# A transformer step's MoE combine: who normalizes the first two tiles, and two rows from TensorE to VectorE

## The chip, the core and the metric

The kernel runs on one core of a Trainium2 chip. A core has five engines that work beside each other: TensorE (PE, matmuls), VectorE (DVE), ScalarE (ACT), GpSimd (POOL) and SyncE (SP, which here issues DMAs). Each runs its own list of instructions in order and waits for the others on semaphores. The metric is the device time of one execution in microseconds (us), as a median of several runs.

## What is computed

The reference is one step of a two-layer backbone on 384 tokens of 1024 numbers: 128 context tokens and 256 latent ones. Each layer has a mixer and a mixture of experts. What the change touches is the end of the second:

```python
xp = _layernorm(ALPHA * xp + mp[5] * _moe(_modulate(xp, mp[3], mp[4]), *mw), ln2_g[l], ln2_b[l])
xs = _layernorm(ALPHA * xs + ms[5] * _moe(_modulate(xs, ms[3], ms[4]), *mw), ln2_g[l], ln2_b[l])

def _layernorm(x, g, b):
    mu = xf.mean(-1, keepdims=True)
    var = jnp.square(xf - mu).mean(-1, keepdims=True)
    y = (xf - mu) * lax.rsqrt(var + LN_EPS) * g + b
...
```

`_moe` sends each token to 8 of 64 experts; its result for a token is the sum of 8 expert rows, each times a weight, and a shared expert's row. In layer 0 what comes next is the mixer of layer 1, which needs the normalized x and its modulated form h, both from the same mean and variance with different scales and shifts. In the last layer the normalized x is the output.

## The kernel before

The tokens are three tiles of 128 (tile 0 is the context). The kernel is written as a sequence of stages; inside a stage each engine has a program written out by hand, and at a stage's end all engines meet. `stage_moe` joins four such programs per engine: routing, experts, overflow and, last, the combine (`combine_programs`, from L3272), once for each layer.

The combine works in this order.

- SP loads the expert rows of each tile back from DRAM (`y_rows`) in six parts, two a tile (L3331). In layer 0 it then loads the first chunks of the next stage's weights, as their places come free (`ahead`). In the last layer it stores the three finished tiles (L3336).
- TensorE sums rows in PSUM banks: first what was placed on chip (L3352), then for each tile some of its 8 rows, each as a product with a diagonal matrix of the weights (L3359), and at the end the part that VectorE summed, as a product with the identity (L3364). Which rows are whose is in the tables `DVE_ROWS` and `PE_ROWS` (L3262). Before, VectorE has 6, 4 and 3 rows of tiles 0, 1 and 2, and TensorE 2, 4 and 5. In layer 0 TensorE then turns tile 0 and tile 1 (`pe_turn_tile`, L1963), runs the first product of the next stage for tile 0 (L509), turns tile 2, and runs tile 1's product.
- VectorE adds its rows into `cat`, each step waiting for the one before (`add_rows`, L3407). `residual(t)` multiplies the sum in PSUM with the gate, in two halves (L3419), and adds it to ALPHA * x (L3422, or L3425 for tile 2). For tiles 0 and 1 this step also gives the sum for the mean (L3428). `centred(t)` is (x + minus mean) * scale over 128x1024 (L3436), and `scaled(t)` is that times rstd plus the shift (L3447), with the result h in `hP`, or in the last layer in x. L3440 makes the variance from the squares, L3449 the small term for the normalized x.
- ScalarE writes the diagonals (L3383) and sums the squares of tiles 0 and 1 (L3388). In layer 0 it copies each turned tile (L1970) and then normalizes x in place (Identity with scale and bias, L3396).
- GpSimd only computes rstd, a power of minus one half on 128x1 (`pool_rstd`, L1941).

Semaphores on the way: `s_mu` mean ready, `s_sq` squares ready, `s_v` variance, `s_p` rstd, `s_h` output of a tile ready (TensorE's turn and SP's store wait for it), `s_sum` and `s_took` for the PSUM banks.

Of the kernel before, what the change touches and what calls it, by code (L numbers as in the profile page):

```python
# [283 lines left out]
def sems(nc, ctx, names):  # L284
    found = [ctx.enter_context(nc.semaphore(n)) for n in names.split()]
    ctx.used += found
    return found
# [2973 lines left out]

DVE_ROWS = ((0, 1, 4, 5, 6, 7), (0, 1, 4, 5), (0, 1, 4))  # L3262
PE_ROWS = tuple(tuple(j for j in range(TOPK) if j not in DVE_ROWS[t]) for t in range(TILES))
# [8 lines left out]
def combine_programs(k, layer, ctx, s_over, s_fold, n_fold, tables, ends, ahead=None):  # L3272
# [34 lines left out]
    def in_place(eng, t, j):  # L3307
# [6 lines left out]
        nc, ctx, "cb_row_added cb_steps cb_var cb_rstd cb_shift cb_h cb_turned outputs_stored")  # L3314
    s_mu, s_sq = sems(nc, ctx, "cb_mean cb_squares")
    squares = k.s[:, 1440:1440 + D]
# [24 lines left out]
    def on_gpsimd(pool):  # L3341
        nc.gpsimd.drain()
        for t in range(TILES):
            pool_rstd(k, M, pool, t, s_v, s_p)

    def on_tensor(pe):
# [33 lines left out]
    def on_scalar(act):  # L3380
        for t in range(TILES):
            for i, j in enumerate(PE_ROWS[t]):
                m = nc.scalar.mul(diag[:, rows_before(PE_ROWS, t) + i, :], k.ident, k.w8[:, t, j:j + 1])  # L3383
            m.then_inc(s_dg, 1)

        def squares_of(t):
            act.wait_ge(s_mu, t + 1)
            nc.scalar.activation(squares, k.x[:, t, :], ACT.Square, bias=M.mv[:, t, 0:1], accum_out=M.mv[:, t, 1:2]).then_inc(s_sq, 1)  # L3388

        squares_of(0)  # L3390
        squares_of(1)
        for t in range(0 if last else TILES):
            x = k.x[:, t, :]
            copy_turned(k, act, t, turn_banks[t], s_tr).then_inc(s_hT, 1)
            act.wait_ge(s_nb, t + 1)
            nc.scalar.activation(x, x, ACT.Identity, bias=M.nb[:, t:t + 1], scale=M.mv[:, t, 1:2])  # L3396

    def on_vector(dve):
        st = Steps(dve, s_d)
        st.mark(nc.vector.memset(M.half, -0.5))  # L3400

        def add_rows(t):
            for i, j in enumerate(DVE_ROWS[t]):
                n = rows_before(DVE_ROWS, t) + i
# [26 lines left out]

        def centred(t):
            G = tables.scale[min(t, 1)]
            if t < SUMMED_BY_ACT:
                dve.wait_ge(s_mu, t + 1)
            st.mark(nc.vector.scalar_tensor_tensor(k.cat[:, t, :], k.x[:, t, :], M.mv[:, t, 0:1], G,  # L3436
                                                   ALU.add if t < SUMMED_BY_ACT else ALU.subtract, ALU.mult))
            if t < SUMMED_BY_ACT:
                dve.wait_ge(s_sq, t + 1)
                nc.vector.tensor_scalar(M.mv[:, t, 1:2], M.mv[:, t, 1:2], 1.0 / D, LN_EPS, ALU.mult, ALU.add).then_inc(s_v, 1)  # L3440

        def scaled(t):
            rstd = M.mv[:, t, 1:2]
            B, out = tables.shift[min(t, 1)], k.x[:, t, :] if last else k.hP[:, t, :]
            st.wait()
            dve.wait_ge(s_p, t + 1)
            nc.vector.scalar_tensor_tensor(out, k.cat[:, t, :], rstd, B, ALU.mult, ALU.add).then_inc(s_h, 1)  # L3447
            if not last:
                nc.vector.tensor_scalar(M.nb[:, t:t + 1], M.mv[:, t, 0:1], rstd, 1.0 if t < SUMMED_BY_ACT else -1.0,  # L3449
                                        ALU.mult, ALU.mult).then_inc(s_nb, 1)  # L3450

        add_rows(0)
        add_rows(1)
        residual(0)
        centred(0)
        residual(1)
        scaled(0)
        centred(1)
        add_rows(2)
        scaled(1)  # L3460
        residual(2)
        centred(2)
        scaled(2)

# [153 lines left out]
```

## Time and profile before

| what | us |
|---|---|
| median of 3 runs (lowest, highest) | 1723.14 (1720.74, 1725.92) |
| the profiled execution | 1723.91 |
| its span, first to last instruction | 1722.0 |
| busy in it: PE, PE weight loads | 1564.6, 739.4 |
| busy in it: DVE, ACT, POOL | 588.9, 368.5, 239.0 |
| combine of layer 0: VectorE's first row, TensorE's first product of the next stage | 883.01, 919.69 |
| combine of the last layer: VectorE's first row, its last step's start | 1677.16, 1717.40 |

The rest of this text reads the trace of the profiled execution. A row of the timeline is: start, duration, engine, line of the kernel, operation, output and inputs by name, their shape, and in brackets for how long the engine had been idle before it and what it waited for. PE's granted clock was 0.961 of full speed over the span.

### The profile page before, as it was taken

The numbers are of one execution on the slowest core, as the hardware profiler recorded it, in microseconds if no ns is written. First come the engines' busy times: TensorE is split into PE (matmuls) and PEld (weight loads), VectorE is DVE, ScalarE is ACT, GpSimd is POOL, SyncE is SP. The second block draws the span as 40 slices with busy tenths as digits, with TensorE's granted clock in tenths as the row PEclk, the third lists the DMA queues.
The fourth block names the chain that finished last, engine by engine and source line by source line (L and its number), as shares of the span: only waits on it lengthen the run. The fifth ranks groups of instructions, "written<-read, shape, count | busy, mean of one in ns | idle before, by whom it ended". The sixth has DMA issues, their size and how long they took to land. (4 is left out here: it accounts for less than half of the span.)

```text
span 1722.0 us, 19372 instructions
## 1 busy us (share of the span) xinstructions
PE 1564.6 (91%) x6918; PEld 739.4 (43%) x6918; DVE 588.9 (34%) x1432; ACT 368.5 (21%) x798; POOL 239.0 (14%) x223
## 2 busy tenths in 40 slices
PE   4999889996898999999999889998698999899987
PEld 1666644542343344344334744533243444344423
DVE  2333685532223111111146675632123111111117
ACT  2224621211111111121224272111011111111121
POOL 0010121111111123111100000111111122211100
PEclk8999999998899999999999999999899999999999
DMA  9990388699999999999983106699999999999974
GB/s 384 374 359 12 137 342 355 244 420 422 399 401 419 400 380 411 396 406 419 380 360 128 62 21 273 270 372 420 412 386 411 389 391 386 406 411 401 400 316 187
DMA packets 110819, 579.55 MB, mean 337 GB/s; under 512 B 22042, under 2 KB 24730, under 8 KB 52480
## 3 DMA queue, kind: packets, MB, share of 16 engines
q1 hardware_dynamic: 87584, 526.61, 75.5%
q0 software_dynamic: 22560, 50.00, 7.6%
q10 hardware_dynamic: 576, 1.66, 0.3%
q8 instruction: 57, 0.93, 0.2%
q14 instruction: 42, 0.34, 0.1%
HBM read 563.77 MB, written 45.30 MB: 354 GB/s over the span
## 5 line engine op out<-in xcount | busy, mean ns | idle before, releaser
L3093 DVE TENSOR_TENSOR scratch<-scratch,bank 128x256 f32<-128x256 f32 x84 | 51.5, 614 | 590.0 <-ACT scratch L3046 561.4
L2952 PE MATMUL bank<-weights,scratch 128*64 128x512 f32 x384 | 185.7, 632 | 52.3 <-DMA scratch<-in_moe_w_up 41.9
L2952 PE MATMUL bank<-scratch 128*64 128x512 f32 x352 | 174.1, 644 | 23.1 <-DMA weights<-in_moe_w_up 14.0
L2953 PE MATMUL bank<-weights,scratch 128*64 128x512 f32 x384 | 190.4, 641 | 0.0
L2953 PE MATMUL bank<-scratch 128*64 128x512 f32 x384 | 185.3, 636 | 0.0
L3046 ACT ACTIVATE scratch<-bank 128x256 f32<-128x256 f32 x84 | 32.2, 383 | 571.5 <-PE bank L2953 355.6
L2952 PEld LDWEIGHTS bank<-weights,scratch 128*64 128x64 f32 x384 | 52.9, 145 | 163.9 <-issue 161.7
L2657 POOL DMA_INDIRECT y_rows<-hP,y_idx x39 | 41.5, 1064 | 448.2 <-ACT hP L3054 330.0
L2952 PEld LDWEIGHTS bank<-scratch 128*64 128x64 f32 x352 | 48.8, 146 | 124.6 <-issue 122.8
L2642 POOL DMA_INDIRECT hP<-h_rows,tok_idx x78 | 81.3, 1043 | 132.8 <-PE bank L2603 66.3
L2959 PE MATMUL bank<-weights,scratch 128*128 128x512 f32 x224 | 98.4, 592 | 0.0
L2959 PE MATMUL bank<-scratch 128*128 128x512 f32 x224 | 98.4, 592 | 0.0
L2990 PE MATMUL bank<-weights,scratch 128*64 128x512 f32 x192 | 87.5, 598 | 2.0 <-ACT scratch L3050 2.0
L2991 PE MATMUL bank<-weights,scratch 128*64 128x512 f32 x192 | 87.5, 599 | 0.0
L2991 PE MATMUL bank<-scratch 128*64 128x512 f32 x192 | 87.5, 599 | 0.0
L2019 PE MATMUL bank<-scratch,cat 128*128 128x512 f32 x192 | 83.7, 594 | 4.1 <-ACT cat L1681 3.4
L2657 POOL DMA_INDIRECT y_rows<-z,y_idx x37 | 39.0, 1055 | 345.2 <-ACT z L3054 269.2
L2990 PE MATMUL bank<-scratch 128*64 128x512 f32 x176 | 80.2, 598 | 3.1 <-ACT scratch L3050 3.1
L2603 PE MATMUL bank<-const,hP 128*128 128x128 f32 x624 | 81.1, 273 | 0.5 <-DMA hP<-h_rows,tok_idx 0.5
L2603 PEld LDWEIGHTS bank<-const,hP 128*128 128x128 f32 x624 | 70.4, 141 | 3.8 <-DMA hP<-h_rows,tok_idx 2.2
L3098 DVE COPY hP<-bank 128x512 f32<-128x512 f32 x40 | 27.7, 692 | 121.7 <-PE bank L2991 121.7
L2959 PEld LDWEIGHTS bank<-scratch 128*128 128x128 f32 x224 | 42.6, 190 | 53.5 <-issue 53.5
(411 smaller groups left out, 2444.5 us busy)
## 6 DMA issues: line engine op xcount, KB each, us to landing
weights<-in_moe_w_gate SPq DMA_DIRECT2D x62, 1024.0 KB, 12.6
weights<-in_moe_w_up SPq DMA_DIRECT2D x62, 1024.0 KB, 20.0
weights<-in_moe_w_down SPq DMA_DIRECT2D x62, 1024.0 KB, 20.6
scratch<-in_moe_w_gate SPq DMA_DIRECT2D x60, 1024.0 KB, 11.9
scratch<-in_moe_w_up SPq DMA_DIRECT2D x60, 1024.0 KB, 20.2
scratch<-in_moe_w_down SPq DMA_DIRECT2D x60, 1024.0 KB, 20.9
weights<-in_w_mod SPq DMA_DIRECT2D x6, 2048.0 KB, 11.3
wmod_more<-in_w_mod SPq DMA_DIRECT2D x6, 2048.0 KB, 8.6
```

Of the source, the lines that this page charges most:

```text
L2019: m = nc.tensor.matmul(k.ps[2 * t + c][:], cat[:, kk, t * P:(t + 1) * P], w_half[c][kk // (KT // 2)][:, kk % (KT // 2), :], start=(kk == 0 ...
L2603: m = k.nc.tensor.transpose(k.ps[kk // 4][:, (kk % 4) * P:(kk % 4 + 1) * P], B.xg[:, b, kk * P:(kk + 1) * P], k.ident)
L2642: return k.nc.gpsimd.indirect_dma_start(out=out, out_offset=None, in_=table, in_offset=bass.IndirectOffsetOnAxis(ap=idx, axis=0), bounds_c ...
L2657: return k.nc.gpsimd.indirect_dma_start(out=table, out_offset=bass.IndirectOffsetOnAxis(ap=idx, axis=0), in_=in_, in_offset=None, bounds_c ...
L2952: nc.tensor.matmul(out[0:HALF, :], x[:, 0:HALF], w0[:, kk], start=(kk == 0), stop=(kk == KT - 1))
L2953: m = nc.tensor.matmul(out[HALF:P, :], x[:, HALF:P], w1[:, kk], start=(kk == 0), stop=(kk == KT - 1))
L2959: m = nc.tensor.matmul(out[:], x, w[:, kk], start=(kk == 0), stop=(kk == KT - 1))
L2990: nc.tensor.matmul(k.ps[5 + c][0:HALF, :], h[:, 0:HALF], w0[:, j, cols], start=(j == 0), stop=(j == 1))
L2991: m = nc.tensor.matmul(k.ps[5 + c][HALF:P, :], h[:, HALF:P], w1[:, j, cols], start=(j == 0), stop=(j == 1))
L3046: nc.scalar.activation(B.ex[b % 2], k.ps[2 + b % 2][:, 0:FD], ACT.Silu).then_inc(s_e, 1)
L3093: nc.vector.tensor_tensor(B.h[b % 2].rearrange("p (j q) -> p q j", j=2), B.ex[b % 2].rearrange("p (q j) -> p q j", j=2), k.ps[2 + b % 2][: ...
L3098: nc.vector.tensor_copy(y_out(b, slice(512, 1024)), k.ps[6][:]).then_inc(s_yv, 1)
```

## The change

For tiles 0 and 1, the two wide VectorE steps `centred` and `scaled` are gone. Instead ScalarE computes the small term (`nb`, minus mean times rstd), waits for it, and normalizes x in place, in both layers; GpSimd multiplies that by the scale and then adds the shift, each over 128x1024, with a semaphore between (`s_xn`, `s_xs`). Tile 2 stays as it was (`normed_last`). VectorE takes one row more of tile 1 and one more of tile 2 (6, 5, 4), TensorE one less of each (2, 3, 4), and VectorE's order is another: the rows of tile 2 come in two pairs around the variance of tile 0, ahead of `residual(1)`. ScalarE's copies of turned tiles come after both normalizations.

```diff
-DVE_ROWS = ((0, 1, 4, 5, 6, 7), (0, 1, 4, 5), (0, 1, 4))
+DVE_ROWS = ((0, 1, 4, 5, 6, 7), (0, 1, 4, 5, 6), (0, 1, 4, 5))
...
         for t in range(TILES):
             pool_rstd(k, M, pool, t, s_v, s_p)
+            if t < SUMMED_BY_ACT:
+                pool.wait_ge(s_xn, t + 1)
+                nc.gpsimd.tensor_tensor(k.cat[:, t, :], k.x[:, t, :], tables.scale[min(t, 1)], ALU.mult).then_inc(s_xs, 1)
+                pool.wait_ge(s_xs, t + 1)
+                nc.gpsimd.tensor_tensor(k.x[:, t, :] if last else k.hP[:, t, :], k.cat[:, t, :], tables.shift[min(t, 1)], ALU.add).then_inc(s_h, 1)
...
-        squares_of(0)
-        squares_of(1)
+        for t in range(SUMMED_BY_ACT):
+            x, rstd = k.x[:, t, :], M.mv[:, t, 1:2]
+            squares_of(t)
+            act.wait_ge(s_p, t + 1)
+            nc.scalar.mul(M.nb[:, t:t + 1], M.mv[:, t, 0:1], rstd).then_inc(s_nb, 1)
+            act.wait_ge(s_nb, t + 1)
+            nc.scalar.activation(x, x, ACT.Identity, bias=M.nb[:, t:t + 1], scale=rstd).then_inc(s_xn, 1)
         for t in range(0 if last else TILES):
+            copy_turned(k, act, t, turn_banks[t], s_tr).then_inc(s_hT, 1)
+        if not last:
+            t = TILES - 1
             x = k.x[:, t, :]
-            copy_turned(k, act, t, turn_banks[t], s_tr).then_inc(s_hT, 1)
...
         add_rows(0)
         add_rows(1)
         residual(0)
-        centred(0)
+        add_rows(2, 0, 2)
+        variance(0)
+        add_rows(2, 2)
         residual(1)
-        scaled(0)
-        centred(1)
-        add_rows(2)
-        scaled(1)
+        variance(1)
         residual(2)
-        centred(2)
-        scaled(2)
+        normed_last()
```

VectorE in the last layer's combine, before, from the mean of tile 0 (L3428) to the rows of tile 2 (L3407):

```order
L3428 TENSOR_SCALAR z<-z 128x1
L3436 SCALAR_TENSOR_TENSOR cat<-x_tok,z,scratch 128x1024
L3440 TENSOR_SCALAR z<-z 128x1
L3419 TENSOR_TENSOR cat<-bank,z 128x512
L3422 SCALAR_TENSOR_TENSOR x_tok,z<-x_tok,cat 128x512
L3419 TENSOR_TENSOR cat<-bank,z 128x512
L3422 SCALAR_TENSOR_TENSOR x_tok,z<-x_tok,cat 128x512
L3428 TENSOR_SCALAR z<-z 128x1
L3447 SCALAR_TENSOR_TENSOR x_tok<-cat,z,scratch 128x1024
L3436 SCALAR_TENSOR_TENSOR cat<-x_tok,z,scratch 128x1024
L3440 TENSOR_SCALAR z<-z 128x1
L3407 SCALAR_TENSOR_TENSOR cat<-scratch,cat 128x1024 x3
```

So each tile's centring and scaling stood on VectorE between the residual steps, and tile 2's rows came after the residual step of tile 1.

The same place in the changed kernel; its L3440 is the mean, L3446 the variance, L3419 a row, L3431 and L3434 the two halves of a residual step:

```order
L3440 TENSOR_SCALAR z<-z 128x1
L3419 SCALAR_TENSOR_TENSOR cat<-scratch,cat 128x1024 x2
L3446 TENSOR_SCALAR z<-z 128x1
L3419 SCALAR_TENSOR_TENSOR cat<-scratch,cat 128x1024 x2
L3431 TENSOR_TENSOR cat<-bank,z 128x512
L3434 SCALAR_TENSOR_TENSOR x_tok,z<-x_tok,cat 128x512
L3431 TENSOR_TENSOR cat<-bank,z 128x512
L3434 SCALAR_TENSOR_TENSOR x_tok,z<-x_tok,cat 128x512
L3440 TENSOR_SCALAR z<-z 128x1
L3446 TENSOR_SCALAR z<-z 128x1
```

Three wide steps (two L3436, one L3447) are gone from between the residual steps, and tile 2's rows, now four, stand ahead of the residual step of tile 1 where three stood behind it.

GpSimd in layer 0's combine, before: the three powers follow each other.

```order
L2657 DMA y_rows<-hP,scratch 3072x1024
L3197 UNCONDITIONAL_BRANCH
L1941 TENSOR_TENSOR z<-z 128x1 x3
L274 UNCONDITIONAL_BRANCH
L562 UNCONDITIONAL_BRANCH
L566 MEMSET z 128x64
L274 UNCONDITIONAL_BRANCH
```

GpSimd had nothing else in this stretch.

And in the changed kernel; L3347 is the product with the scale, L3349 the sum with the shift:

```order
L2657 DMA y_rows<-hP,scratch 3072x1024
L3197 UNCONDITIONAL_BRANCH
L1941 TENSOR_TENSOR z<-z 128x1
L3347 TENSOR_TENSOR cat<-x_tok,z 128x1024
L3349 TENSOR_TENSOR hP<-cat,z 128x1024
L1941 TENSOR_TENSOR z<-z 128x1
L3347 TENSOR_TENSOR cat<-x_tok,scratch 128x1024
L3349 TENSOR_TENSOR hP<-cat,scratch 128x1024
L1941 TENSOR_TENSOR z<-z 128x1
L274 UNCONDITIONAL_BRANCH
```

Two wide steps stand between the powers of tiles 0 and 1, and two between those of tiles 1 and 2.

## Rows read from the trace of the kernel before

**Rows 1.** The page's head: span and number of instructions.
```profile
span 1722.0 us, 19372 instructions
```

**Rows 2.** Groups by line and shape, VectorE's rows: count, busy us, mean ns, idle us.
```profile
L3407 DVE SCALAR_TENSOR_TENSOR cat<-scratch,cat 128x1024 f32<-128x1024 f32 x14 | 18.0, 1283 | 1.3
```

**Rows 3.** Timeline of the last layer's combine, VectorE and GpSimd's powers: start, duration.
```profile
1677.16 2.68 DVE L3407 SCALAR_TENSOR_TENSOR cat<-weights,scratch,cat 128x1024 f32<-128x1024 f32 x2
...
1685.51 5.45 DVE L3407 SCALAR_TENSOR_TENSOR cat<-weights,scratch,cat 128x1024 f32<-128x1024 f32 x4
1691.67 0.69 DVE L3419 TENSOR_TENSOR cat<-bank,z 128x512 f32<-128x512 f32 x1 [0.72 <-PE bank L3364]
...
1696.36 0.56 POOL L1941 TENSOR_TENSOR z<-z 128x1 f32<-128x1 f32 x1 [41.48 <-DVE z L3440]
...
1705.66 4.06 DVE L3407 SCALAR_TENSOR_TENSOR cat<-scratch,cat 128x1024 f32<-128x1024 f32 x3
1705.83 1.52 POOL L1941 TENSOR_TENSOR z<-z 128x1 f32<-128x1 f32 x1 [8.91 <-DVE z L3440]
...
1717.40 1.28 DVE L3447 SCALAR_TENSOR_TENSOR x_tok<-cat,z,scratch 128x1024 f32<-128x1024 f32 x1 [0.52 <-POOL z L1941]
```

**Rows 4.** Timeline of layer 0's combine and the next stage, VectorE and TensorE.
```profile
883.01 2.69 DVE L3407 SCALAR_TENSOR_TENSOR cat<-weights,scratch,cat 128x1024 f32<-128x1024 f32 x2
...
915.96 1.28 DVE L3447 SCALAR_TENSOR_TENSOR hP<-cat,z,scratch 128x1024 f32<-128x1024 f32 x1
...
917.92 1.91 PE L1963 MATMUL bank<-const,hP 128*128 128x128 f32 x16
919.69 7.13 PE L509 MATMUL bank<-weights,hT 128*128 128x512 f32 x16
...
935.14 7.10 PE L509 MATMUL bank<-weights,hT 128*128 128x512 f32 x16 [0.58 <-PEq L274]
```

**Rows 5.** Timeline of layer 0's combine, TensorE: tile 1's rows and sum, tile 2's sum.
```profile
898.45 7.03 PE L3359 MATMUL bank<-weights,scratch 128*128 128x512 f32 x16
905.32 1.88 PE L3364 MATMUL bank<-cat,const 128*128 128x512 f32 x4
...
916.10 1.99 PE L3364 MATMUL bank<-cat,const 128*128 128x512 f32 x4 [0.33 <-DVE cat L3407]
```

**Rows 6.** SP's issues in layer 0's combine; DMA issues: KB each, median us to landing.
```profile
882.44 2.25 SPq L3331 DMA_DIRECT2D scratch<-y_rows  x3
...
scratch<-y_rows SPq DMA_DIRECT2D x2, 1024.0 KB, 18.5
```

**Rows 7.** Timeline near 190 us: a VectorE step with GpSimd idle, and beside it.
```profile
183.85 0.17 DVE L1317 TENSOR_SCALAR scratch<-scratch 128x4 f32<-128x4 f32 x1
...
194.57 0.45 POOL L1920 TENSOR_TENSOR cat<-cat 16x128 f32<-16x128 f32 x1
194.71 0.33 DVE L1317 TENSOR_SCALAR scratch<-scratch 128x4 f32<-128x4 f32 x1
```

**Rows 8.** Timeline of the last layer's combine, ScalarE's squares and their read.
```profile
1694.84 1.15 ACT L3388 ACTIVATE scratch<-x_tok,z 128x1024 f32<-128x1024 f32 x1 [13.62 <-DVE z L3428]
1695.90 0.19 ACT L3388 ACTIVATION_READ_ACCUMULATOR scratch<-x_tok,z 128x1 f32 x1
```

**Rows 9.** Groups by line and shape: GpSimd's wide product, ScalarE's Identity.
```profile
L1948 POOL TENSOR_TENSOR x_tok<-x_tok,scratch 128x1024 f32<-128x1024 f32 x12 | 28.3, 2362 | 0.3
...
L3396 ACT ACTIVATE x_tok<-x_tok,z 128x1024 f32<-128x1024 f32 x3 | 3.8, 1257 | 0.0
```

**Rows 10.** Timeline, TensorE after two long waits: first slow and first fast step.
```profile
1324.25 1.09 PE L2952 MATMUL bank<-weights,scratch 128*64 128x512 f32 x1 [4.87 <-DMA weights<-in_moe_w_up]
...
1327.60 0.59 PE L2952 MATMUL bank<-weights,scratch 128*64 128x512 f32 x1
...
700.72 1.08 PE L2952 MATMUL bank<-scratch 128*64 128x512 f32 x1 [4.22 <-DMA scratch<-in_moe_w_up]
...
706.50 0.59 PE L2952 MATMUL bank<-scratch 128*64 128x512 f32 x1
```

More of the change, by code:

```diff
@@ L3314, in combine_programs @@
         nc, ctx, "cb_row_added cb_steps cb_var cb_rstd cb_shift cb_h cb_turned outputs_stored")
-    s_mu, s_sq = sems(nc, ctx, "cb_mean cb_squares")
+    s_mu, s_sq, s_xn, s_xs = sems(nc, ctx, "cb_mean cb_squares cb_x_normed cb_x_scaled")
     squares = k.s[:, 1440:1440 + D]
@@ L3400, in on_vector, with add_rows @@
         st.mark(nc.vector.memset(M.half, -0.5))
-        def add_rows(t):
-            for i, j in enumerate(DVE_ROWS[t]):
+        def add_rows(t, lo=0, hi=TOPK):
+            for i, j in list(enumerate(DVE_ROWS[t]))[lo:hi]:
                 n = rows_before(DVE_ROWS, t) + i
@@ L3430, in residual, with variance, normed_last @@
                 dve_variance(k, M, st, t, s_v)
[L3432 to L3442, printed above, removed]
+        def variance(t):
+            dve.wait_ge(s_sq, t + 1)
+            nc.vector.tensor_scalar(M.mv[:, t, 1:2], M.mv[:, t, 1:2], 1.0 / D, LN_EPS, ALU.mult, ALU.add).then_inc(s_v, 1)
+        def normed_last():
+            t = TILES - 1
             rstd = M.mv[:, t, 1:2]
-            B, out = tables.shift[min(t, 1)], k.x[:, t, :] if last else k.hP[:, t, :]
+            st.mark(nc.vector.scalar_tensor_tensor(k.cat[:, t, :], k.x[:, t, :], M.mv[:, t, 0:1], tables.scale[1], ALU.subtract, ALU.mult))
             st.wait()
             dve.wait_ge(s_p, t + 1)
-            nc.vector.scalar_tensor_tensor(out, k.cat[:, t, :], rstd, B, ALU.mult, ALU.add).then_inc(s_h, 1)
+            dve.wait_ge(s_h, t)
+            nc.vector.scalar_tensor_tensor(k.x[:, t, :] if last else k.hP[:, t, :], k.cat[:, t, :], rstd, tables.shift[1],
+                                           ALU.mult, ALU.add).then_inc(s_h, 1)
             if not last:
-                nc.vector.tensor_scalar(M.nb[:, t:t + 1], M.mv[:, t, 0:1], rstd, 1.0 if t < SUMMED_BY_ACT else -1.0,
-                                        ALU.mult, ALU.mult).then_inc(s_nb, 1)
+                dve.wait_ge(s_nb, t)
+                nc.vector.tensor_scalar(M.nb[:, t:t + 1], M.mv[:, t, 0:1], rstd, -1.0, ALU.mult, ALU.mult).then_inc(s_nb, 1)
         add_rows(0)
```

## The prediction

> **What bounds the kernel now.** I read the chain that ended last first, then the two stretches of the combine stage engine by engine in order of time, then the boundary to the next stage. The span is 1722.0 us [rows 1]. Most of it is TensorE and weight DMA, which the change does not touch; it touches two stretches of some 40 us, one per layer.
>
> In both, VectorE sets the pace at first: row after row of 1.28 us [rows 2], started every 1.39 us ((5.45 - 1.28) / 3, from the run of four [rows 3]). After that the layers differ. In the **last layer** the end of the program is VectorE's last step, which ends at 1718.68 [rows 3]; the store takes the rest, 3.3 us. In **layer 0** nothing waits for VectorE's last step. TensorE does: it turns tiles 0 and 1 from 917.92, starts the first product at 919.69, and from there goes on with at most 0.58 us of idle time into the next stage [rows 4]. So layer 0 is paid by the moment at which TensorE may turn tile 1, and the last layer by the end of tile 2. Each is added to the span in full.
>
> **The change, part by part**, in layer 0's clock. The last layer runs the same code 794.15 us later (rows start at 883.01 and at 1677.16) [rows 3, 4].
>
> *Rows moved.* TensorE loses one row from tile 1 and one from tile 2. Four rows take it 16 records, 905.32 - 898.45 = 6.87 us, so 1.72 us a row [rows 5]. Tile 1's sum moves from 905.3 to 903.6, tile 2's is possible at 903.6 + 1.7 + 4 x 1.72 = 912.2, where it began at 916.1 and waited for VectorE's rows [rows 5]. VectorE gains two rows, 2.8 us, but loses four wide steps of 1.28 us (centring and scaling of tiles 0 and 1). Its eleven rows now end at 883.01 + 10 x 1.39 + 1.28 = 898.2. The residual step of tile 0 takes 3.17 us until ScalarE starts its squares on the mean (1691.67 to 1694.84 [rows 3, 8]): mean at 901.4. Two rows of tile 2 until 904.2, the variance at 904.4. The last two rows read the last part of y_rows: issued near 884.3 and 18.5 us in landing [rows 6], it is there at 902.8, so they don't wait; 904.4 to 907.1. VectorE by itself would have tile 2 done much earlier than now.
>
> *The new path of a tile.* From the variance: GpSimd's rstd, ScalarE's shift and Identity, GpSimd's product and sum. Rstd is seen at 0.56 and at 1.52 us; the long one has a VectorE row running beside it [rows 3, 7]. Tile 0's has one too: 1.52, to 906.0. The shift is a 128x1 step on ScalarE; the nearest is its 0.19 read [rows 8], I take 0.2. Identity over 1024 columns is the same form as the one timed at 1.26 us [rows 9]. ScalarE is done at 907.5. A GpSimd product of 128x1024 is in the trace, 12 times, 2.36 us [rows 9]; the new ones have the same operands and shape. Tile 0 needs two: 4.7 us on GpSimd in place of 2.6 us on VectorE.
>
> *Who shares with whom.* This decides the case. At 194.57 GpSimd runs a product of 0.45 us, until 195.02. VectorE's scalar step that starts at 194.71 lasts 0.33 us, to 195.04, where the same step takes 0.17 us with GpSimd idle [rows 7]. And rstd's long form ends 0.4 us after the VectorE row beside it. So each holds the other up until it is done. No wide GpSimd step of the trace has a two-input VectorE step beside it, so the size is bounded: from nothing to all of what is left of the 2.36 us. I take the whole, as the rows nearest to it show a full block.
> [...]
>
> *Tile 0 with exclusion.* GpSimd's product runs 907.6 to 910.0. VectorE's residual step of tile 1 begins at 907.2 with a product out of PSUM (0.69), then asks at 907.9 for its step over two SBUF tensors. It waits until 910.0, ends at 910.7. GpSimd's sum, ready at 910.1, runs 910.7 to 913.0. VectorE's second such step, ready at 911.6, waits until 913.0, ends at 913.7. Mean of tile 1 at 914.0: VectorE lost 2.1 + 1.4 = 3.5 us.
>
> *Tile 1.* Squares on ScalarE 1.25 us (1694.84 to 1696.09 [rows 8]), variance at 915.5, rstd 0.57 to 916.1, shift and Identity to 917.8. GpSimd's product 917.9 to 920.3; VectorE's second two-input step of tile 2, ready at 918.4, goes 920.3 to 921.0; GpSimd's sum 921.0 to 923.3. Before, tile 1's output was there at 915.96 + 1.28 = 917.24 [rows 4].
>
> *What waits.* In layer 0 TensorE turns tile 0 at about 914 and then waits for tile 1 until 923.4; ahead of the first product it still needs 0.9 us (half of 1.91 [rows 4]), so that starts at 924.3 against 919.69: **+4.6 us**. Queued behind that wait stand both early products and the turn of tile 2, and behind them the stage's end, for which all engines wait. ScalarE's copies of tile 0 are done by 918.9 and tile 2 is ready before its turn: no further cost. The three loads of the next weights on SP now go out some 1.7 us earlier and hide as before.
> *The clock.* TensorE stands idle from about 915 to 923.4. [...] I take the middle, **+2.3 us**.
> *Last layer.* Tile 1 is there at 923.3 + 794.15 = 1717.5. VectorE's centring of tile 2 waits for it and runs to 1718.7; rstd comes 0.4 us behind, the last step ends at 1720.6 instead of 1718.68: **+1.9 us**.
> Sum 4.6 + 2.3 + 1.9 = 8.8 us. The profiled execution took 1723.91 us, 0.8 above the median 1723.14; 1732.7 there is 1731.9 on the median.
>
> **Rivals.**
> *VectorE first.* GpSimd's product of tile 0 has 0.3 us of head start (907.6 against 907.9), made of four handovers that I took at 0.1 us. Later by more than that, VectorE takes its step first, GpSimd runs 908.6 to 910.9, VectorE loses 1.5 us in tile 1 in place of 3.5, tile 1 is done at 921.7 and the last step of the last layer 0.2 us sooner than before. 2.9 + 2.3 - 0.2 = 5 us: 1728.1.
> *No exclusion for these steps; not slower.* VectorE's mean of tile 1 comes at 910.2, its variance at 911.7. GpSimd is busy with tile 0 until 912.3, then rstd, ScalarE, and 4.8 us more: 919.5. TensorE is +0.7 us, idle 4.5 us, so the clock's 2.3 stays; in the last layer the last step ends at 1715.7, -3.0. Sum 0: 1723.1, and 1720.8 if the clock holds. It decides if the two-input steps run on beside GpSimd. For it: the only blocked VectorE steps in sight are single-input ones. Against it: it is two-input rows behind which rstd waits.
> *More collisions.* If the small VectorE steps (means, accumulator reads) are held too, or wide GpSimd steps take longer beside VectorE, each of the four wide pairs costs 0.5 to 1 us more: +11 to 13 us, about 1735.
>
> **How the numbers follow.** Exclusion with GpSimd first 0.47 (1729.5 to 1734, the clock's 1.7 to 2.9 and handovers in it), VectorE first 0.20, no exclusion 0.20, more collisions 0.13. 0.3% is 5.2 us, so slower means above 1728.3: 0.45 of the first, 0.09 of the second, all of the last, 0.67. Faster, below 1718, would need the third case with the clock kept and a shorter rstd: 0.03. Same 0.30. The range takes in the first two, half the third and most of the fourth: 1723 to 1735.
>
> **What would show it.** In the profile after: the two-input residual steps of tile 1 and tile 2 last 2 to 3 us instead of 0.69, and end when a GpSimd step ends; tile 1's turn in layer 0 starts near 923.4 after some 8 us of idle time; the first product's steps come at 1.06 us for some us; the last VectorE step ends near 1720.6. I am wrong if those steps stay at 0.69 us (then 1723), if the turn comes before 920, or if something outside the two combines moves, which nothing here foresees.

## The result and the profile after

The changed kernel takes 1729.2 us in the median of 14 runs (1724.8 to 1734.3), the kernel before 1722.9 us beside it (14 runs). The ratio is 1.0037, 95% interval [1.0027, 1.0047]: 6.3 us slower, where 8.8 was forecast. The profiled execution of the changed kernel took 1729.3 us, its span is 1727.8 against 1722.0 [rows 1].

```profile
span 1727.8 us, 19344 instructions
...
PE 1549.8 (90%) x6902; PEld 735.4 (43%) x6902; DVE 594.2 (34%) x1426; ACT 371.6 (22%) x800; POOL 257.8 (15%) x231
```

That is the head of the page after. Work moved as intended: GpSimd has 19 us more. VectorE has 5 us more, although in each layer it lost four wide steps (5.1 us) and got only two rows (2.6 us). The timeline of VectorE in layer 0's combine tells why (start, duration, engine, line, operation, tiles, shape, idle time before it in brackets):

```profile
897.99 4.06 DVE L3419 SCALAR_TENSOR_TENSOR cat<-weights,scratch,cat 128x1024 f32<-128x1024 f32 x3 [1.13 <-DMA weights<-y_rows]
...
904.15 0.69 DVE L3434 SCALAR_TENSOR_TENSOR x_tok<-x_tok,cat 128x512 f32<-128x512 f32 x1
...
907.94 2.67 DVE L3419 SCALAR_TENSOR_TENSOR cat<-scratch,cat 128x1024 f32<-128x1024 f32 x2 [0.19 <-DMA scratch<-y_rows]
...
911.25 2.13 DVE L3434 SCALAR_TENSOR_TENSOR x_tok<-x_tok,cat 128x512 f32<-128x512 f32 x1
...
913.42 0.69 DVE L3431 TENSOR_TENSOR cat<-bank,z 128x512 f32<-128x512 f32 x1
914.15 2.00 DVE L3434 SCALAR_TENSOR_TENSOR x_tok<-x_tok,cat 128x512 f32<-128x512 f32 x1
...
920.67 2.38 DVE L3437 SCALAR_TENSOR_TENSOR x_tok<-x_tok,cat 128x512 f32<-128x512 f32 x1
...
924.13 2.21 DVE L3451 SCALAR_TENSOR_TENSOR cat<-x_tok,z,scratch 128x1024 f32<-128x1024 f32 x1
```

GpSimd at the same time:

```profile
907.84 0.57 POOL L1941 TENSOR_TENSOR z<-z 128x1 f32<-128x1 f32 x1 [40.86 <-DVE z L3446]
910.09 2.73 POOL L3347 TENSOR_TENSOR cat<-x_tok,z 128x1024 f32<-128x1024 f32 x1 [1.69 <-ACT x_tok L3401]
912.90 2.68 POOL L3349 TENSOR_TENSOR hP<-cat,z 128x1024 f32<-128x1024 f32 x1
917.94 0.55 POOL L1941 TENSOR_TENSOR z<-z 128x1 f32<-128x1 f32 x1 [2.35 <-DVE z L3446]
920.17 2.34 POOL L3347 TENSOR_TENSOR cat<-x_tok,scratch 128x1024 f32<-128x1024 f32 x1 [1.68 <-ACT x_tok L3401]
922.59 2.67 POOL L3349 TENSOR_TENSOR hP<-cat,scratch 128x1024 f32<-128x1024 f32 x1
```

The centring of tile 2 in the kernel before:

```profile
921.95 1.28 DVE L3436 SCALAR_TENSOR_TENSOR cat<-x_tok,z,scratch 128x1024 f32<-128x1024 f32 x1
```

The residual step over two SBUF tensors (L3434, L3437) takes 0.69 us for tile 0, with GpSimd idle, and 2.13, 2.00 and 2.38 us where GpSimd has a wide step running. GpSimd's product runs from 910.09 to 912.82 and VectorE's 911.25 step ends at 913.38, 0.56 us later. Its neighbours that read PSUM (L3431) stay at 0.69 us throughout. The blocking goes both ways. The product of tile 0 begins at 910.09 while VectorE's rows run until 910.61, and takes 2.73 instead of some 2.35 us. The sum of 912.90 begins while VectorE's residual step still runs and takes 2.68. The centring of tile 2 takes 2.21 instead of 1.28 us.

What is blocked in these wide rows finishes 0.1 to 0.2 us sooner than a start at the other's end would let it (a residual step 0.54 to 0.57 us behind its blocker against 0.69, the centring 1.08 against 1.28). GpSimd's power on 128x1 is no such case: it runs from 907.84 to 908.41, and VectorE's rows, which start at 907.94, are not held (2.67 us for two, as ever).

TensorE in layer 0, from the turn of tile 0 to the turn of tile 2:

```profile
916.73 1.04 PE L1963 MATMUL bank<-const,hP 128*128 128x128 f32 x8
925.40 1.94 PE L1963 MATMUL bank<-const,hP 128*128 128x128 f32 x8 [7.64 <-POOL hP L3349]
927.14 8.83 PE L509 MATMUL bank<-weights,hT 128*128 128x512 f32 x16
935.80 1.04 PE L1963 MATMUL bank<-const,hP 128*128 128x128 f32 x8
```

The turn of tile 2 in the kernel before, where the first product starts at 919.69 [rows 4]:

```profile
926.66 1.04 PE L1963 MATMUL bank<-const,hP 128*128 128x128 f32 x8
```

TensorE has the wait of the forecast, 7.64 us for GpSimd's sum of tile 1. Then eight small products take 1.94 us instead of 1.04, and the first product, until the next turn, 8.66 us instead of 6.97. The granted clock says why. Two stretches of the changed kernel, the turn and the product (length, busy time and instructions of PE, PEld, DVE, ACT, POOL, granted clock, DMA share, GB/s):

```profile
925.40:927.10 1.70, 1.70 (x8) 1.70 (x9) 1.19 (x2) 0.57 (x1) 1.35 (x1) 0.50 0.00 0
927.15:935.80 8.65, 8.65 (x17) 3.67 (x17) 1.11 (x2) 0.59 (x1) 0.00 (x0) 0.79 0.01 2
```

It is 0.50 of full speed over the turn and 0.79 over the product. In the kernel before it is 1.00 over both.

From here on a time "in" a combine counts from VectorE's first row there: 885.85 and 1683.31 us after, 883.01 and 1677.16 before.

| place | before | after | difference |
|---|---|---|---|
| first row of layer 0's combine, absolute | 883.01 | 885.85 | +2.8 |
| TensorE's first product (L509), in the combine | 36.68 | 41.29 | +4.6 |
| turn of tile 2 behind it | 43.65 | 49.95 | +6.3 |
| last product group of that stretch (L509) | 52.13 | 58.44 | +6.3 |
| from there to the last layer's first row | 742.02 | 739.02 | -3.0 |
| last VectorE step's start, in the last combine | 40.24 | 39.84 | -0.4 |

The first and the fifth line lie where nothing was changed; the profiles below spread by more than that there (881 to 889.6 us for the first line, 736.5 to 745.1 for the fifth), and here they cancel (2.8 - 3.0). What is left is 6.3 - 0.4 = 5.9 us, near the 6.3 of the medians. All of the loss is in layer 0.

### The profile page after: what moved, and what is told of

The parts are those of the page before. It is cut to its first block and busy times, and to the rows that moved or that the text cites. A ratio compares the mean times of both kernels' runs of the same rounds, so it can differ in the third digit from the quotient of the medians.

```text
span 1727.8 us, 19344 instructions
## 1 busy us (share of the span) xinstructions
PE 1549.8 (90%) x6902; PEld 735.4 (43%) x6902; DVE 594.2 (34%) x1426; ACT 371.6 (22%) x800; POOL 257.8 (15%) x231
## 5 line engine op out<-in xcount | busy, mean ns | idle before, releaser
L2952 PE MATMUL bank<-weights,scratch 128*64 128x512 f32 x384 | 184.5, 628 | 53.2 <-DMA scratch<-in_moe_w_up 44.4
L2952 PE MATMUL bank<-scratch 128*64 128x512 f32 x352 | 167.0, 622 | 27.9 <-DMA weights<-in_moe_w_up 15.5
L2953 PE MATMUL bank<-weights,scratch 128*64 128x512 f32 x384 | 183.8, 622 | 0.0
L2953 PE MATMUL bank<-scratch 128*64 128x512 f32 x384 | 182.4, 627 | 0.0
L2952 PEld LDWEIGHTS bank<-weights,scratch 128*64 128x64 f32 x384 | 52.5, 144 | 163.7 <-issue 161.7
L2952 PEld LDWEIGHTS bank<-scratch 128*64 128x64 f32 x352 | 47.3, 142 | 125.5 <-issue 123.5
L2990 PE MATMUL bank<-weights,scratch 128*64 128x512 f32 x192 | 87.5, 598 | 2.0 <-ACT scratch L3050 2.0
L2991 PE MATMUL bank<-scratch 128*64 128x512 f32 x192 | 87.5, 598 | 0.0
L2991 PE MATMUL bank<-weights,scratch 128*64 128x512 f32 x192 | 87.5, 598 | 0.0
L2990 PE MATMUL bank<-scratch 128*64 128x512 f32 x176 | 80.2, 598 | 3.1 <-ACT scratch L3050 3.1
```

Source lines behind the costliest of these rows:

```text
L2952: nc.tensor.matmul(out[0:HALF, :], x[:, 0:HALF], w0[:, kk], start=(kk == 0), stop=(kk == KT - 1))
L2953: m = nc.tensor.matmul(out[HALF:P, :], x[:, HALF:P], w1[:, kk], start=(kk == 0), stop=(kk == KT - 1))
L2990: nc.tensor.matmul(k.ps[5 + c][0:HALF, :], h[:, 0:HALF], w0[:, j, cols], start=(j == 0), stop=(j == 1))
L2991: m = nc.tensor.matmul(k.ps[5 + c][HALF:P, :], h[:, HALF:P], w1[:, j, cols], start=(j == 0), stop=(j == 1))
```

## The experiments

Twelve more runs were made, each timed beside the kernel before. An expectation is quoted, then the measured. All short diffs are against the changed kernel unless they say otherwise.

**The changed kernel again.** No edit.

> The changed kernel once more, unaltered, for a second profile. The theory (GpSimd's wide steps and VectorE's two-input steps exclude each other, and TensorE's clock falls in the longer wait for tile 1) expects +6.3 us against the kernel before. In the first profile VectorE also waited 1.13 us for y_rows in layer 0's combine, which the kernel before did not. If that was chance it is gone here, and tile 1's turn starts about 38.5 us after VectorE's first row instead of 39.55. Rival: the wait for y_rows belongs to the change and is there again.

1.0054 [1.0037, 1.0071]. In its profile the first product starts at 41.01, the last product group at 58.53, the last VectorE step at 39.84: the same picture as in the table, to 0.3 us.

**The gated sum stays in PSUM.** VectorE's residual step then has one SBUF and one PSUM input. TensorE's turn waits for the mean (`s_mu`) instead.

```diff
-nc.vector.tensor_tensor(f[:, cols], k.ps[2 * t + c][:], tables.gate[...][:, cols], ALU.mult)
+nc.vector.tensor_tensor(k.ps[2 * t + c][:], k.ps[2 * t + c][:], tables.gate[...][:, cols], ALU.mult)
-nc.vector.scalar_tensor_tensor(x[:, cols], x[:, cols], ALPHA, f[:, cols], ...)
+nc.vector.scalar_tensor_tensor(x[:, cols], x[:, cols], ALPHA, k.ps[2 * t + c][:], ...)
```

> The changed kernel, but the gated sum f is written back to its PSUM bank instead of to SBUF, so that the residual step of VectorE reads one SBUF tensor and one PSUM tensor, not two SBUF tensors. Durations alone stay the same. Exclusion theory: the residual steps of tiles 1 and 2 that took 2.13, 2.00 and 2.38 us take 0.69 again, the mean of tile 1 comes 2.7 us earlier, GpSimd is then the one that is late, tile 1 is finished 2.4 us earlier in both layers, and the time is +1.5 us against before (range 0 to 3), some 4.8 us under the changed kernel. Rival (GpSimd's wide steps only take long by themselves, 2.4 us each in series, and the long VectorE steps have another cause): nothing moves, +6.3 us.

1.0012 [0.9997, 1.0026]. VectorE's timeline there, tile 1's two residual steps, and GpSimd's two wide steps of tile 0 beside them:

```profile
909.41 0.69 DVE L3434 SCALAR_TENSOR_TENSOR x_tok<-x_tok,bank 128x512 f32<-128x512 f32 x1
...
910.87 0.69 DVE L3434 SCALAR_TENSOR_TENSOR x_tok<-x_tok,bank 128x512 f32<-128x512 f32 x1
```

```profile
908.25 2.73 POOL L3347 TENSOR_TENSOR cat<-x_tok,z 128x1024 f32<-128x1024 f32 x1 [1.69 <-ACT x_tok L3401]
911.06 2.35 POOL L3349 TENSOR_TENSOR hP<-cat,z 128x1024 f32<-128x1024 f32 x1
```

The same step, at the same moment, beside the same GpSimd work, is back at 0.69 us, and GpSimd's sum at 2.35. So it is the second SBUF input that collides. (The product still takes 2.73 us: it meets VectorE's last row, which has two SBUF inputs as before.) The turn of tile 1 comes at 36.25 instead of 39.55, 3.3 us sooner where 2.4 were expected, and layer 0 is 3.4 us shorter (last product group at 55.09); some 0.3 us of that are a shorter y_rows wait (0.84 against 1.13). In the last layer this profile shows no gain, its last step starts at 39.80, but 3.3 us of y_rows waits lie in it; the last experiment shows that layer without them. TensorE's 4.33 us wait still costs the clock: turn 1.94 us, first product 8.78 us.

**Useless products between the turns.** Eight more matrix products in layer 0, whose result nobody reads, between TensorE's turns of tile 0 and tile 1.

```diff
             turn(0)
+            pe.wait_ge(s_took, 2)
+            pe_keep_warm(k, 0, 8)
             turn(1)
```

> The changed kernel with 8 matmuls of no use (16 records of 0.43 us) on TensorE in layer 0 between the turns of tile 0 and tile 1, where it stood idle 7.6 us. Clock theory: the turn of tile 1 takes 0.9 us instead of 1.74 and the first product's 16 records 7.0 us instead of 8.7, so 2.6 us of the 6.3 go: +3.7 us against before. Rival (the next stage waits for something else by then, so TensorE's slow records cost nothing): +6.3 us.

1.0033 [1.0019, 1.0047]. TensorE there:

```profile
916.26 7.03 PE L1954 MATMUL bank<-const 128*128 128x512 f32 x16
923.13 1.04 PE L1963 MATMUL bank<-const,hP 128*128 128x128 f32 x8
924.00 7.03 PE L509 MATMUL bank<-weights,hT 128*128 128x512 f32 x16
930.87 1.04 PE L1963 MATMUL bank<-const,hP 128*128 128x128 f32 x8
```

The turn is at 1.04 and the first product at 7.03 us, as before the change. From the turn's start to the next turn it is 7.74 us instead of 10.40, so the clock's price in the changed kernel is 2.66 us (2.56 against the kernel before: 0.87 in the turn, 1.69 in the product). The granted clock is 1.00 over turn and product here. Layer 0 is 3.6 us shorter than in the changed kernel, 2.7 from the clock, the rest because VectorE had no y_rows wait there in this profile. The last layer was 2.6 us longer, with 2.8 us of such waits (below), which is why the time shows so little.

**GpSimd's wide steps cut to one column.** The scaling and the shift of tiles 0 and 1 are left out, but for their first column; every wait stays.

```diff
-nc.gpsimd.tensor_tensor(k.cat[:, t, :], k.x[:, t, :], tables.scale[...], ALU.mult)
+nc.gpsimd.tensor_tensor(k.cat[:, t, 0:1], k.x[:, t, 0:1], tables.scale[...][:, 0:1], ALU.mult)
```

> The changed kernel with GpSimd's product and sum of tiles 0 and 1 cut to one column each: the scaling and shifting of these two tiles is left out. All waits stay. What is left is the moved rows, the new order on VectorE and ScalarE's normalization. Theory: TensorE turns tile 1 right behind tile 0, the first product starts 3.4 us earlier than before, in the last layer the last VectorE step starts 3.9 us earlier: about -7 us against before. Rival (the moved rows or VectorE's new order cost time): it stays at or above the time before.

0.9964 [0.9949, 0.9979]. The last product group starts at 48.39, 3.7 us before that of the kernel before, and the last VectorE step at 36.31, 3.9 us before. With the work of GpSimd gone and all else of the change in place, the kernel is 6 us faster than before. The whole loss is therefore GpSimd's 4.7 us a tile and what it does to its neighbours; order, semaphores and rows are not to blame.

**The rows alone**, on the kernel before.

```diff
-DVE_ROWS = ((0, 1, 4, 5, 6, 7), (0, 1, 4, 5), (0, 1, 4))
+DVE_ROWS = ((0, 1, 4, 5, 6, 7), (0, 1, 4, 5, 6), (0, 1, 4, 5))
```

> The kernel before with only the two rows moved from TensorE to VectorE (6, 5, 4), its order and normalization kept. Worked out: tile 1's sum is ready 1.7 us earlier and VectorE waited 3.9 us for it, tile 2 has one VectorE row of 1.39 us more: -0.3 us a layer, -0.6 in all, no change that can be told (-2 to +1). Rival (each added row is on VectorE's path in full): +2.8 us a layer, +5.6.

1.0025 [1.0011, 1.0039]: some 4 us slower, outside what was expected. Layer 0 did as expected (last product group at 51.81, -0.3). The last layer did not: its last step starts at 42.08, +1.8, and the timeline of VectorE shows a wait that the profile of the kernel before has nowhere:

```profile
1688.29 4.06 DVE L3407 SCALAR_TENSOR_TENSOR cat<-weights,scratch,cat 128x1024 f32<-128x1024 f32 x3 [3.02 <-DMA weights<-y_rows]
```

**The normalization alone**: the changed kernel with the old rows (the diff above, reversed).

> The changed kernel with the rows as before (6, 4, 3). VectorE reaches tile 1's residual step 2.8 us earlier, but TensorE's sum of tile 1 is 1.7 us later and becomes the limit. By the theory GpSimd's product of tile 0 is then under way when VectorE asks, as now. I expect tile 1 within 1 us of the changed kernel's and the same time within 2 us: +4.5 to +7 us. Rival (the moved rows are what costs): near 0.

1.0037 [1.0022, 1.0052], the same as the whole change. The last product group starts at 56.07 (+3.9 against the kernel before), the last step at 40.82 (+0.6). The rows shift 1 to 2.4 us between the layers and are worth nothing in sum that the times show (in the traces 1.4 us). TensorE waited 2.77 us here and its first product took 8.03 us.

**Tile 0 on ScalarE and GpSimd, tile 1 on VectorE** as before the change.

```diff
-            if t < SUMMED_BY_ACT:
+            if t == 0:
                 pool.wait_ge(s_xn, t + 1)
...
         residual(1)
+        centred(1)
         variance(1)
+        scaled(1)
```

> The changed kernel, but tile 1 is centred and scaled on VectorE as before, and only tile 0 goes over ScalarE and GpSimd. ScalarE normalizes tile 1 behind its copies. Theory: VectorE still waits for tile 0's two GpSimd steps (about 2.7 us), but tile 1 no longer waits for them a second time: its output is there 33 to 35 us after VectorE's first row instead of 39.5, at or before the time of the kernel before (34.2), TensorE has no long wait, no slow clock; the last layer gains 0.5 to 1 us. In all -2 us against before (-4 to +1). Rival (it is tile 0's pair of steps that costs, through VectorE's waits): +3 or more.

1.0009 [0.9994, 1.0025]: no gain where about -2 us was expected. Layer 0 is shorter than before the change (50.53, -1.6); TensorE waits only 2.12 us and its next turn takes 1.06 us. The last layer is 1.9 us longer, again with y_rows waits, 3.1 us in three places.

**The same with the sum in PSUM.**

> As the run with only tile 0 on GpSimd, and f in PSUM so that the residual steps don't collide. Exclusion theory: only VectorE's centring of tile 1 can still meet tile 0's sum on GpSimd. Tile 1 is there 1 to 2 us sooner than without it: -4 us against before (-6 to -1). Rival (no exclusion): the same as that run.

0.9986 [0.9973, 0.9999], -2.4 us, inside the expectation though short of its -4. Layer 0 is 4.0 us shorter than before the change (48.10), the last layer 0.8 us longer with 3.5 us of y_rows waits.

Whose are these waits? Five profiles had up to 3.5 us of them in the last layer and all five have the moved rows, so the rows were under suspicion. The last four kernels went for that.

**The kernel before, unchanged.**

> The kernel before, unchanged, for a second profile of it and for the spread of the comparison. Its ratio should be 1.000 within 0.0015. The question is the wait for y_rows. Theory A: it belongs to the moved rows, VectorE asks for the third part too early only with them; then VectorE's idle time ended by the y_rows transfers is 0 in both combines here, as in the first profile of this kernel. Theory B: it belongs to the execution. [...]

1.0012 [0.9996, 1.0027]. A kernel against itself: so much a comparison of this kind can be off, some 2 us. In layer 0 its profile has a y_rows wait, without a moved row:

```profile
897.93 2.67 DVE L3407 SCALAR_TENSOR_TENSOR cat<-weights,scratch,cat 128x1024 f32<-128x1024 f32 x2 [0.90 <-DMA weights<-y_rows]
900.89 0.69 DVE L3419 TENSOR_TENSOR cat<-bank,z 128x512 f32<-128x512 f32 x1 [0.29 <-PE bank L3364]
```

The last layer has none, and its granted clock from 1655 to 1660 us, some 5 us ahead of the loads, was 0.72 (0.83 over the 10 us ahead of them). The wait in layer 0 cost nothing: the first product starts at 36.67, as in the first profile, since VectorE waits 0.29 us for TensorE's sum behind it instead of 1.09.

**The rows alone, again.**

> The kernel before with only the two rows moved from TensorE to VectorE, once more. In the first such run it was 1.0025 [1.0011, 1.0039] against an expected -0.6 us. Theory A (the two rows themselves cost, through VectorE's wait for y_rows): again 1.002 to 1.003, +3 to +5 us, with a y_rows wait of 1 to 3 us in the last layer. Theory B (the execution): the ratio comes nearer to 1, within 0.9990 to 1.0015, and the last layer's last VectorE step starts 40.2 us plus the y_rows wait of that profile after the first row. Layer 0's first product is again 0.3 us sooner than before by either.

1.0012 [0.9999, 1.0026], the same as the unchanged kernel beside it. Layer 0 is 0.3 us shorter, the last step starts at 40.05, 0.2 us before that of the kernel before, with 1.92 us of y_rows wait in it. By the time this is theory B: the two rows cost nothing beside the unchanged kernel, and the two runs of the same kernel, 1.0025 and 1.0012, show how far such ratios spread. By the step it is neither: theory B had 40.2 us plus the wait, 42.1, and the 1.92 us did not show in the end at all. In the first profile of this kernel 3.02 us of wait went with a last step 2.0 us later (42.08). So such a wait costs only what is not covered by waits that VectorE had anyway.

**Tile 0 on GpSimd, sum in PSUM, old rows.**

> Tile 0 on ScalarE and GpSimd, tile 1 on VectorE, the gated sum left in PSUM (as in the fourth kernel of the last call, 0.9986 [0.9973, 0.9999]), but with the old rows 6, 4, 3. If the moved rows cost 2 to 4 us by themselves (theory A), this one is 0.9965 to 0.998, -4 to -6 us against the kernel before. If they cost nothing (theory B), it is 0.998 to 0.9995, -1 to -3 us, and layer 0's first product starts 32.7 to 34.4 us after VectorE's first row, with up to 1.7 us for the row that TensorE has again in tile 1.

0.9992 [0.9977, 1.0008]. The first product starts at 36.08, late even for the 1.7 us allowed for. TensorE comes to its turns at 34.32 and does both in one go: with the old rows its own sums set the moment, 3.4 us (two rows of 1.72) later than with the moved ones, and what tile 0's path won is idle. In the last layer the old rows are the better ones by 1.3 us. So the rows give in one layer and take in the other, as in the normalization alone (there with the signs reversed: the moved rows cost 2.4 us in layer 0 and gave 1.0 in the last). And this kernel, with the old rows, has the longest y_rows waits of all in its last layer, on VectorE:

```profile
1685.66 2.67 DVE L3420 SCALAR_TENSOR_TENSOR cat<-weights,scratch,cat 128x1024 f32<-128x1024 f32 x2 [1.98 <-DMA weights<-y_rows]
...
1696.09 1.28 DVE L3420 SCALAR_TENSOR_TENSOR cat<-scratch,cat 128x1024 f32<-128x1024 f32 x1 [2.04 <-DMA scratch<-y_rows]
```

So the waits need no moved rows, and the changed kernel, with moved rows, had none in the last layer in either profile. What tells the profiles apart is when SP's first load of y_rows goes out, and the granted clock a few us ahead of it. First this kernel, then the kernel before of two sections above (columns of a stretch: length, busy time and instructions of PE, PEld, DVE, ACT, POOL, granted clock, DMA share, GB/s):

```profile
1655.00:1660.00 5.00, 5.00 (x26) 1.92 (x26) 0.00 (x0) 1.17 (x2) 0.06 (x1) 1.00 0.54 211
...
1662.98 0.34 SPq L3331 DMA_DIRECT2D weights<-y_rows  x1
```

```profile
1655.00:1660.00 5.00, 2.94 (x8) 1.05 (x10) 0.00 (x0) 0.27 (x1) 1.00 (x1) 0.72 0.77 277
...
1664.78 0.34 SPq L3331 DMA_DIRECT2D weights<-y_rows  x1
```

Over the 10 us ahead of the first load the last expert products (L2952, L2953) take 0.60 us each in the first, at a granted clock of 1.00, and VectorE's first row follows 9.7 us behind that load (1672.66 - 1662.98). In the second they take 0.72 us at a clock of 0.83, and the row follows 12.6 us behind (1677.34 - 1664.78). The six parts (12.6 MB) come one behind the other, in the five stretches of 5 us from 1668 to 1693 us at 408 to 442 GB/s in the first and at 398 to 451 in the second; by these rates they take some 29 us, an estimate. In 14 profiles the distance is 9.2 to 9.8 us seven times, each time with 1.9 to 4.0 us of y_rows waits in the last layer, and 12.6 to 14.5 us seven times, never with one. Over the 10 us ahead of the first load the granted clock is 1.00 in each of the first seven and 0.66 to 0.83 in each of the others. So the waits go with the clock of the last expert products, with old rows as with moved ones, and what these gain at full clock the combine gives back in part. That the kernel has no say in it is not shown: three kernels were profiled twice, and each came out on the same side both times (before 14.0 and 12.6 us, the change 14.2 and 13.1, the rows alone 9.6 and 9.8).

**Both remedies on the changed kernel**: sum in PSUM and useless products.

> The changed kernel with both remedies: the gated sum left in PSUM, so that VectorE's residual steps have one SBUF input and do not meet GpSimd, and eight products with no use on TensorE between the turns of tile 0 and tile 1 in layer 0. The PSUM form alone was 1.0012, the useless products alone 1.0033, the change 1.0037 to 1.0054. The turn of tile 1 took 1.94 us and the first product 8.78 us in the PSUM form; both fall to 1.04 and 7.03, so layer 0 is 2.6 us shorter than there and the ratio 0.9990 to 1.0005. If the idle time between the turns (4.33 us) is too short for the useless products to fit, they push the turn by up to 1 us and the gain is 1.5 us.

1.0006 [0.9991, 1.0022], just above what was expected and not to be told from the PSUM form alone. The eight useless products run from 916.58 to 923.45, until 38.6 in the combine, where tile 1 was ready at 36.2: they pushed the turn by 2.4 us and gained 2.6. Layer 0 ends at 54.86 against 55.09. By these rows four (3.4 us) would have fitted; that was not tried.

The last layer of this kernel is that of the PSUM form, here without y_rows waits:

```profile
1718.63 1.28 DVE L3457 SCALAR_TENSOR_TENSOR x_tok<-cat,z,scratch 128x1024 f32<-128x1024 f32 x1 [0.51 <-POOL z L1941]
```

It starts 36.81 us after VectorE's first row, 3.0 us sooner than in the changed kernel and 3.4 sooner than before the change. So the sum in PSUM is worth 3 us in the last layer too, where no y_rows wait hides it. The change with both remedies is then level with the kernel before, -0.7 us in the trace and +1.0 [-1.5, 3.8] in time: what it wins in the last layer (-3.4), layer 0 takes back (+2.7).

All kernels, as traced and as timed. "Traced" is the shift of the last product group in layer 0 plus that of the last step in the last layer, against the first profile of the kernel before; "timed" is the ratio less 1, times 1722 us.

| kernel | layer 0 | last layer | y_rows waits, last layer | traced | timed |
|---|---|---|---|---|---|
| the change | +6.3 | -0.4 | 0 | +5.9 | +6.4 [4.6, 8.1] |
| the change again | +6.4 | -0.4 | 0 | +6.0 | +9.3 [6.4, 12.2] |
| sum in PSUM | +3.0 | -0.4 | 3.3 | +2.5 | +2.1 [-0.5, 4.5] |
| useless products | +2.7 | +2.2 | 2.8 | +4.9 | +5.7 [3.3, 8.1] |
| one column | -3.7 | -3.9 | 0 | -7.7 | -6.2 [-8.8, -3.6] |
| rows alone | -0.3 | +1.8 | 3.0 | +1.5 | +4.3 [1.9, 6.7] |
| normalization alone | +3.9 | +0.6 | 0 | +4.5 | +6.4 [3.8, 9.0] |
| tile 0 only | -1.6 | +1.9 | 3.1 | +0.3 | +1.5 [-1.0, 4.3] |
| tile 0, PSUM | -4.0 | +0.8 | 3.5 | -3.2 | -2.4 [-4.6, -0.2] |
| before, again | 0.0 | 0.0 | 0 | 0.0 | +2.1 [-0.7, 4.6] |
| rows alone, again | -0.3 | -0.2 | 1.9 | -0.5 | +2.1 [-0.2, 4.5] |
| tile 0, PSUM, old rows | -0.6 | -0.5 | 4.0 | -1.1 | -1.4 [-4.0, 1.4] |
| PSUM and useless products | +2.7 | -3.4 | 0 | -0.7 | +1.0 [-1.5, 3.8] |

The order is nearly the same in both columns. No kernel here beats the one before by more than its interval and the 2 us of the unchanged kernel together, save the one that leaves work out. The best of the whole ones, tile 0 on GpSimd with the sum in PSUM, is at -2.4 us.

## Why the prediction was right, and where its sum was not

*Exclusion, GpSimd first.* Right, and the first rival's other order did not come. In all profiles of the changed kernel GpSimd's product starts ahead of VectorE's step: 910.09 against 911.25, 1706.53 against 1707.56. The head start was forecast at 0.3 us and is 1.0 to 1.2, for the most part because the rstd before it took 0.95 us less. What the prediction did not have is that the product itself meets VectorE's last row and is held by it for 0.3 to 0.4 us.

The time alone would not have told this case from its first rival: +6.3 us lies nearer to the rival's 5 than to 8.8, and 1729.2 just below the 1729.5 to 1734 that the prediction gave to this case. The profile tells them apart. The row from which the prediction took its full block (0.33 against 0.17 us) is of a VectorE step with one input, so it showed that something holds, not what a step with two inputs loses; the rows above do that.

*The first product, +4.6 us.* Measured +4.6, but by chance: three terms were off and cancel. VectorE waited 1.13 us for y_rows in layer 0, where the prediction looked only at the last part of them and had no wait. (For the last part it had none either, and it was 0.19.) In the kernel before such a wait is covered by the idle time in which VectorE waits for TensorE's sums, 1.09 us at tile 0 and 3.89 at tile 1:

```profile
897.89 0.69 DVE L3419 TENSOR_TENSOR cat<-bank,z 128x512 f32<-128x512 f32 x1 [1.09 <-PE bank L3364]
...
906.37 0.69 DVE L3419 TENSOR_TENSOR cat<-bank,z 128x512 f32<-128x512 f32 x1 [3.89 <-PE bank L3364]
```

In the changed kernel VectorE's eleventh row (1.39 us) fills the first, and the rows of tile 2 ahead of the residual step of tile 1 fill the second. So the wait is on the path: 1.13 us with the turn of tile 1 at 39.55, 0.83 us with 39.28 in the repeat, and none with tile 1 ready at 38.27 in the kernel with useless products. Without the wait tile 1 is ready 2.0 us sooner than the sum had it (38.3 against 40.3): 0.6 us up to the variance of tile 0; 0.95 in its rstd, below; and 0.45 from there, where each blocked step ends 0.1 to 0.2 us sooner than the prediction had it, less the 0.3 us for which VectorE's row holds the product. And the turn itself ran at half clock, 1.94 us for eight products, where the prediction counted 0.9 and began the clock's price only behind it.

*The clock, +2.3 us.* No run shows this term; it was the author's estimate, the middle of 1.7 and 2.9 us, half of the 3.35 and 5.8 us for which the steps of [rows 10] stay slow (1.09 and 1.08 us at first, 0.59 after it). The runs showed 2.6 in its place, at a granted clock of 0.50 over the turn and 0.79 over the product; 0.9 of it stands in the first product's start above. So layer 0 is +6.3 where 4.6 + 2.3 = 6.9 was forecast. Across the kernels the time from the start of tile 1's turn to the next turn, less the 7.74 us of the kernel with useless products, is 0.0 us after 2.12 us of idle time, 1.7 after 2.77, 2.6 after 4.33, 3.0 after 7.37 (the repeat) and 2.7 after 7.64. From 4.33 us on it hardly grows, so cutting 3 us of the wait bought nothing from the clock.

*The last layer, +1.9 us.* Wrong: -0.4. This is the term that made 8.8 out of 6. The first step of it that failed is "The long one has a VectorE row running beside it. Tile 0's has one too: 1.52". VectorE's row and GpSimd's power start almost together, 1704.23 and 1704.28, and the power takes 0.56 us:

```profile
1704.23 2.69 DVE L3419 SCALAR_TENSOR_TENSOR cat<-scratch,cat 128x1024 f32<-128x1024 f32 x2
```

```profile
1704.28 0.56 POOL L1941 TENSOR_TENSOR z<-z 128x1 f32<-128x1 f32 x1 [43.15 <-DVE z L3446]
...
1721.53 1.52 POOL L1941 TENSOR_TENSOR z<-z 128x1 f32<-128x1 f32 x1
```

The long one starts later in a VectorE step, 1.09 us into it here and 0.17 us in [rows 3]. That VectorE has a step running is not enough: in all 14 profiles the power takes 0.54 to 0.57 us where it starts from 0.13 us ahead of a two-input SBUF step of VectorE to 0.05 us behind its start, and 1.51 to 1.53 where it starts 0.16 us or more behind. Beside a step that reads PSUM (L3431, 0.16 us behind its start) it takes 0.55. The second failed step is VectorE's loss of 3.5 us in tile 1: it is 1.43 + 1.30 = 2.7 us, since GpSimd was ready sooner and both blocked steps end 0.54 us behind it. Tile 1 is then ready at 38.25 (1721.56 - 1683.31) and not at 40.3: 0.5 us by the variance of tile 0, 0.95 by its rstd, 0.6 over the handovers. That is 2.1 of the 2.3 us between +1.9 and -0.4.

*No further cost on ScalarE and SP, the stages outside.* Right: 2.8 and -3.0 us lie outside the combines and cancel, and the other profiles scatter there more. TensorE's idle time ahead of the stage's next group (L509) is 0.58 us before and after.

*The rivals.* "No exclusion" is out by the 2.13 us rows. "More collisions" is out too, its small steps (accumulator reads, means) stay at 0.08 and 0.21 us; but its wide half was partly true: GpSimd's steps take 2.6 to 2.7 us beside VectorE and 2.34 to 2.36 alone, some 0.3 us in three of four a layer, hidden by the sooner start.

*What stays open.* Why the timed differences lie above the traced ones, by 1.4 us in the mean of the 13, the unchanged kernel too. One profile is one execution, and the y_rows waits alone move it by 2 us. Open too is why the clock ahead of the last combine is full in some executions and not in others.

## What to carry to other kernels

Here, moving wide elementwise work from VectorE to GpSimd freed VectorE only where its steps at that time had at most one SBUF input. If they have two, these runs say that either their order has to keep the engines apart or one operand should stay in PSUM: that alone was worth 3.4 us in layer 0, and 3.0 in the last layer where no y_rows wait hid it. It does not make GpSimd's path shorter: two steps of 2.35 us stand there for two of 1.28 on VectorE, and whoever waits for the tile pays that. And before a row, a tile or a step is moved off the engine that waits, look for waits that its idle time covers: a transfer that ends 1 us later than it should is seen only when the cover is gone.

## What the runs showed of the hardware

- A two-input SBUF step of VectorE (128x512, 0.69 us alone) took 1.99 to 2.38 us in the changed kernel beside a GpSimd step of 128x1024; with one input in PSUM it took 0.69 us at the same moment. Blocked, it ended 0.54 to 0.57 us behind its blocker. A blocked GpSimd step of 128x1024 took 2.6 to 2.7 there instead of 2.35 us, and 3.33 in the last layer of the kernel with the sum in PSUM, where it started 0.18 us after a VectorE row.
- A GpSimd step of 128x1 that started 0.05 us after a VectorE row was not held (0.56 to 0.57 us); 0.16 us after it or later it was (1.51 to 1.53 us). It did not hold a VectorE row that started 0.10 us behind it.
- TensorE paid for a pause of 4.33 us about as much as for one of 7.64 us (2.6 and 2.7 us, 3.0 for 7.37), 1.7 us for 2.77 us, and nothing for 2.12 us. The granted clock from the turn to the next turn was 0.74 after 7.64 us, 0.72 after 7.37, 0.75 after 4.33, 0.82 after 2.77 and 1.00 after 2.12.
- In 14 profiles, where the granted clock was 1.00 over the 10 us ahead of the last layer's first y_rows load, the first row of the combine came 9.2 to 9.8 us behind that load and VectorE waited 1.9 to 4.0 us for y_rows; where it was 0.66 to 0.83, the row came 12.6 to 14.5 us behind and VectorE did not wait.
